# Attention branches D, B and C: where a modulation sum, A's turned outputs and the next branch's operands stand in a step

## Chip, cores and metric

The kernel runs on one core of a Trainium2 chip. The metric is the device time of one execution in microseconds (us), as a median over runs. Engines are named as in the profile: PE is TensorE, DVE is VectorE, ACT is ScalarE, POOL is GpSimd and SP is the queue that starts the weight transfers.

## What is computed

Two layers of a hybrid backbone over 256 latent and 256 context tokens, all in float32. Of a layer this matters here:

```python
out_a = mlstm_output(h_lat, mo, m_norm_g)          # branch A: normalised, gated
out_b = global_attention(...)                      # B: RMS-normed, rotated q and k
out_c = window_attention(..., sink)                # C: rotated q and k, sink logits
out_d = neighbourhood_attention(..., rel_bias)     # D: bias by relative position
# merge_branches:
g = jax.nn.sigmoid(gate_raw.reshape(B, T, N_BRANCH, D_MODEL))
y = g[:, :, 0] * (branches[0] @ w_branch[0])
for i in range(1, N_BRANCH):
    y = y + g[:, :, i] * (branches[i] @ w_branch[i])
return y @ w_out
```

After it comes a mixture of 32 experts with a modulation of its own. The modulation row is `silu(c) @ w_mod + b_mod`, one row per layer, of which the blocks n = 4 to 11 (512 columns each) are worked out beside the attention branches.

## The kernel before

The branches of a layer run in the order A, D, B, C. A stage is a list of items: in D, B and C an item is a pair of heads by 128 queries, 16 items in layer 0 and 8 in layer 1 (which needs the 256 latent tokens alone). A stage has one step more than items. In step i the engines do the following, each in its own program order, tied by semaphores:

- PE: `turn(i-1)` transposes the probabilities of item i-1 (L1373), `scores(i)` (L1363) multiplies queries and keys of the next, then come "dense groups" that belong to no item, with `values(i-1)` (L1387) between their two halves.
- DVE: `peaks(i)` adds the bias (L2075; at some items of D after four operations at L2067) and takes the maxima (L2078, L2084), `normalise(i)` scales the exponentials (L2096, L2098), `outputs(i-1)` copies the item's result (L2106).
- ACT: `turned_copy(i-1)` (L1085), `exponentials(i)` (L1096), then `fill`, which evacuates the dense groups that are ACT's (L953).

The dense groups are spread over the steps by `due`: projections for the next branch (`gq`, `gkv` in D, `wq`, `wkv` in B; L1213), products of the previous branch's outputs with `w_branch` (`val`, L1327; evacuated by DVE at L1915 and L1917, or L1919 and L1921) and gates (`gate`, L1314; evacuated by ACT). They take turns in two PSUM banks: group g writes bank g modulo 2 and waits until group g-2 has been evacuated (`dense_free`). Every engine knows a group's number from `plan_dense`, which lists the groups in order. A step has one or two groups in layer 0 and two or three in layer 1.

Three pieces of work beside the items are what the change touches.

- **Modulation sums.** In B and C, DVE adds up `csil * w_mod` row by row at the end of each step (`accumulate`, L1941 and L1943, four operations a step). When a block is complete, `modulation_sum` lets PE add over the partitions (L1231), a dense group too, and `sum_rows` lets DVE add the bias row (L1959). In layer 0 they stand in steps 4, 8, 12 and 16 of B and of C, in layer 1 in steps 2, 4, 6 and 8.
- **A's outputs.** DVE ends A with a norm over its outputs (L1881 to L1895) and raises `o_ready`. PE's `out_transposed("A")` waits for it and transposes them (L1249, four groups in layer 0, two in layer 1), and ACT evacuates them to where D's `val` groups read them.
- **The next branch.** `prepare_normed(i)` in D and `prepare_plain(i)` in B let DVE square, norm and rotate the operands of B and of C (L2013, L2014, L2019 to L2030, L1976 to L1981) once they have been evacuated. From step 8 of D in layer 0, and from step 5 in layer 1, a step norms and rotates one operand part or two.

Of the kernel before, what the change touches and what calls it, by code (L numbers as in the profile page):

```python
# [31 lines left out]
D = 1024  # L32
# [93 lines left out]
HOLD = {"A": 2}  # L126
PAIRS = 4
# [54 lines left out]
def sums_at(l, b, i):  # L182

    return [j for j in range(len(sum_blocks(l, b))) if sum_span(l, b, j)[1] == i]
# [46 lines left out]
def plan_dense():  # L231

    order = []
    for l in range(L):
        qt = q_tiles(l)
# [3 lines left out]
        for b in STAGES:  # L239
            n = n_items(l, b)  # L240
            after = {"D": "B", "B": "C"}.get(b)
            for i in range(stage_steps(l, b)):
                if b == "A" and i < n and spread_head(l, i) is not None:
                    order += [(l, "cb", 2 * spread_head(l, i) + d) for d in range(2)]
                if after and i == n:
                    order += [(l, "qt" + after, t) for t in range(qt)] + [(l, "kt" + after, 0)]
                order += [(l, "sum" + b, j) for j in sums_at(l, b, i)]
                order += [(l,) + fill_groups(l, b)[k] for k in due(l, b, i)]
            if b == "A":
                order += [(l, "otA", t) for t in range(qt)]  # L250
# [22 lines left out]
def hybrid_moe_kernel(nc, ins, out):  # L273
# [3 lines left out]
    with ctx:  # L277
# [667 lines left out]
        def _(act):  # L945
# [12 lines left out]
            for l in range(L):  # L958
# [113 lines left out]
                out_transposed("A")  # L1072

                def attention(b, sqrt_at=None):
# [25 lines left out]
                    for i in range(n + 1):  # L1100
# [7 lines left out]
                        if i == n and b in "DB":  # L1108
                            operands_transposed("B" if b == "D" else "C")
                        fill(b, i)  # L1110
# [74 lines left out]
        def _(pe):  # L1185
# [34 lines left out]
            for l in range(L):  # L1220
# [128 lines left out]
                def pairs(b):  # L1349
# [41 lines left out]
                    for i in range(n + 1):  # L1391
# [6 lines left out]
                        for j in sums_at(l, b, i):  # L1398
                            modulation_sum(b, j)
                        groups = due(l, b, i)  # L1400
                        half = (len(groups) + 1) // 2
                        fill(b, groups[:half])
                        if i:
                            values(i - 1)
# [60 lines left out]
                out_transposed("A")  # L1465
# [231 lines left out]
        def _(dve):  # L1697
# [34 lines left out]
            for l in range(L):  # L1732
# [314 lines left out]
                def attention(b):  # L2047
# [60 lines left out]
                    for i in range(n + 1):  # L2108
                        if i < n:
                            peaks(i)  # L2110
                        if b == "D":
                            prepare_normed(i)
                        if b == "B":
                            prepare_plain(i)
                        if i < n:
                            normalise(i)
                        sum_rows(b, i)
                        groups = due(l, b, i)
                        half = (len(groups) + 1) // 2
                        fill(b, groups[:half])  # L2120
                        if i:
                            outputs(i - 1)
# [289 lines left out]
```

How the kernel before makes its waits and increments, by code:

```python
        def weights(eng, key):  # L630
            slot, count, width = BLOCK[key]
            eng.wait_ge(w_full[slot], count)
            return slot_view(slot, width)
# [1 line left out]
        def expert_weights(eng, l, slot, i, width):  # L636
            eng.wait_ge(w_full[slot], 16 * first_use[l, slot] + 16 * i)
            return slot_view(slot, width)
# [9 lines left out]
        def wait_alone(eng, *waits):  # L649
            for s, v in waits:
                eng.wait_ge(s, v)
            eng.sem_inc(passed, 1)
# [7 lines left out]
            def __call__(self, ins_):  # L661
                ins_.then_inc(self.s, 1)
                self.n += 1
                self.eng.wait_ge(self.s, self.n)
# [1 line left out]
        def dense_wait(eng, g):  # L666
            eng.wait_ge(dense_full, g + 1)
            return ps[g % N_DENSE]
# [4 lines left out]
        @block.sync  # L674
        def _(sp):
            sp.dma_start(craw[:, 0, :], ins["c"]).then_inc(c_loaded, 16)
            sp.dma_start(craw[:, 1, :], ins["c_ctx"]).then_inc(c_loaded, 16)
            sp.dma_start(X[0:HALF, :, :], ins["x"][0].rearrange("(t p) d -> p t d", p=HALF)).then_inc(x_loaded, 16)
            sp.dma_start(X[HALF:P, :, :], ins["ctx"][0].rearrange("(t p) d -> p t d", p=HALF)).then_inc(x_loaded, 16)
            for l in range(L):
                for dst, src, wait, arrived in blocks[l]:
                    if wait:
                        sp.wait_ge(*wait)
                    sp.dma_start(dst, src).then_inc(arrived, 16)
                def load_expert(c, e, par):
```

## Time and profile before

| | |
|---|---|
| median of 3 runs | 2915.06 us (2908.91 to 2915.38) |
| the profiled execution | 2908.26 us, span 2906.8 us |
| PE busy | 2524.3 us, 87% of the span |
| chain that ended last, by engine | PE 67%, DMA 16%, DVE 9% |
| DVE, ACT busy | 1059.6 and 487.1 us |
| granted TensorE clock, mean | 0.939 |

In the profiled execution the stages D, B and C of layer 0 lie between 400 and 952 us, those of layer 1 between 1925 and 2254 us. A row of the time line has start, length, engine, line and operation, and in brackets how long its engine sat idle before it and what released it. A matmul in float32 shows as two records, so eight products are `x16`.

### The profile page before, as it was taken

What the parts mean: (1) busy time and instruction counts of PE and PEld (TensorE: products, weight loads), DVE (VectorE), ACT (ScalarE), POOL (GpSimd) and SP (SyncE); (2) the same over time, 40 slices, a digit from 0 to 9 for tenths busy, and PEclk for the clock granted to TensorE, in tenths of its full rate; (3) what the DMA queues carried; (4) which work ended last, traced back from release to release, by engine and by line L of the source; (5) the groups of instructions that cost most, each with busy time, mean ns of one, the idle gap of its engine ahead of it and who ended that gap; (6) DMA issues with size and microseconds to landing.
All of it is one profiled execution on the core that took longest, in us unless ns stands there. A gap on an engine that the chain in (4) does not pass through costs nothing.

```text
span 2906.8 us, 45309 instructions
## 1 busy us (share of the span) xinstructions
PE 2524.3 (87%) x18912; PEld 1544.5 (53%) x18913; DVE 1059.6 (36%) x2421; ACT 487.1 (17%) x965; POOL 251.5 (9%) x426
## 2 busy tenths in 40 slices
PE   5999989998889859999999789998989758888871
PEld 2455545454444457777777456566666434444440
DVE  1206536256474322222222332435446422111115
ACT  1113222222221100101001112222222101101010
POOL 3000000000000011111111200000001021111111
PEclk9989999999999959999999998999999879999996
DMA  9181202132325439999999721122455659999992
GB/s 291 58 328 49 68 34 69 48 134 84 102 95 141 162 114 367 372 372 385 382 378 386 258 92 58 58 102 84 156 167 147 253 197 408 412 417 411 411 378 81
DMA packets 153888, 618.46 MB, mean 213 GB/s; under 512 B 17680, under 2 KB 22080, under 8 KB 136960
## 3 DMA queue, kind: packets, MB, share of 16 engines
q1 hardware_dynamic: 126944, 558.92, 51.2%
q0 software_dynamic: 21696, 37.26, 4.8%
q10 hardware_dynamic: 5152, 20.97, 1.8%
q8 instruction: 64, 1.05, 0.1%
q14 instruction: 32, 0.26, 0.0%
HBM read 600.12 MB, written 46.32 MB: 222 GB/s over the span
## 4 chain that ended last, share of the span: by engine, by line
PE 67%; DMA 16%; DVE 9%; issue 4%; ACT 2%; ACTq 1%; POOL 1%; SPq 0%; DVEq 0%; POOLq 0%
DMA ring<-in_e_down_dram 13%; PE bank L1565 12%; PE bank L1314 12%; PE bank L1213 10%; PE bank L1203 6%; PE score_banks L1582 4%; PE bank L1327 3%; PE score_banks L1602 3%; PE score_banks L1587 2%; PE bank L1484 2%; PE score_banks L1363 2%; PE turned_banks L1373 2%; PE bank L1387 2%; PE bank L1242 1%; PE bank L1548 1%
## 5 line engine op out<-in xcount | busy, mean ns | idle before, releaser
L1565 PEld LDWEIGHTS bank<-scr,ring 128*64 128x64 f32 x8192 | 341.2, 138 | 14.7 <-issue 14.7
L1565 PE MATMUL bank<-scr,ring 128*64 128x96 f32 x8192 | 347.4, 247 | 1.4 <-DVE scr L2258 1.2
L1314 PE MATMUL bank<-HT,ring 128*128 128x512 f32 (+1 forms) x1024 | 343.9, 491 | 0.0
L1213 PE MATMUL bank<-ring,HT 128*128 128x512 f32 (+1 forms) x800 | 303.7, 536 | 5.9 <-ACT ring L953 5.9
L1558 PE MATMUL bank<-ring,scr 128*64 128x256 f32 x2048 | 238.4, 386 | 43.2 <-DMA ring<-in_e_gate_dram 21.6
L1314 PEld LDWEIGHTS bank<-HT,ring 128*128 128x128 f32 x1024 | 190.7, 190 | 141.8 <-issue 129.4
L1213 PEld LDWEIGHTS bank<-ring,HT 128*128 128x128 f32 x800 | 151.8, 193 | 150.9 <-issue 138.2
L1558 PEld LDWEIGHTS bank<-ring,scr 128*64 128x64 f32 x2048 | 146.5, 139 | 138.1 <-DMA ring<-in_e_gate_dram 38.2
L1203 PE MATMUL bank<-HT,ring 128*128 128x512 f32 (+1 forms) x512 | 197.6, 545 | 5.1 <-ACT scr L953 3.6
L1602 PE MATMUL score_banks<-ring,scr 128*64 128x512 f32 x512 | 135.2, 676 | 37.8 <-DMA ring<-in_e_down_dram 36.2
L1203 PEld LDWEIGHTS bank<-HT,ring 128*128 128x128 f32 x512 | 97.7, 193 | 96.7 <-issue 90.6
L953 ACT ACTIVATE ring<-bank 128x512 f32<-128x512 f32 (+1 forms) x122 | 63.1, 521 | 501.1 <-PE bank L1314 274.8
L1166 ACT ACT_TABLE_LOAD x64 | 82.1, 1283 | 348.9 <-DVE scr L2276 170.7
L1166 ACT ACTIVATE scr<-bank 128x384 f32<-128x384 f32 (+1 forms) x64 | 28.0, 438 | 634.2 <-PE bank L1565 336.1
L1582 PE MATMUL score_banks<-ring,scr 128*64 128x512 f32 x512 | 116.9, 598 | 0.8 <-issue 0.8
L1943 DVE SCALAR_TENSOR_TENSOR scr<-ring,csil,scr 128x512 f32<-128x512 f32 x160 | 109.9, 744 | 0.2
L2276 DVE TENSOR_TENSOR scr<-scr,bank 128x384 f32<-128x384 f32 x32 | 17.7, 554 | 248.9 <-PE bank L1565 248.9
L1096 ACT ACTIVATE scr<-score_banks,nms 128x512 f32<-128x512 f32 (+1 forms) x144 | 87.0, 609 | 113.1 <-DVE nms L2084 113.1
L1548 PE MATMUL bank<-consts,scr 96*128 96x96 f32 (+1 forms) x512 | 71.5, 282 | 39.2 <-DMA scr<-h,idx 19.6
L1242 PE MATMUL bank<-ring,scr 128*128 128x512 f32 x128 | 64.0, 662 | 47.5 <-DMA ring<-in_w_mod_dram 27.2
L1373 PE MATMUL turned_banks<-consts,scr 128*128 128x128 f32 x480 | 71.0, 290 | 37.3 <-DVE scr L2098 37.2
L2078 DVE TENSOR_REDUCE nm<-score_banks 128x2 f32<-128x1024 f32 (+1 forms) x72 | 75.2, 1044 | 72.4 <-PE score_banks L1363 70.3
(243 smaller groups left out, 2727.0 us busy)
## 6 DMA issues: line engine op xcount, KB each, us to landing
ring<-in_e_up_dram SPq DMA_DIRECT2D x64, 2048.0 KB, 21.1
ring<-in_e_down_dram SPq DMA_DIRECT2D x64, 2048.0 KB, 19.8
ring<-in_e_gate_dram SPq DMA_DIRECT2D x64, 2048.0 KB, 19.9
ring<-in_w_in_dram SPq DMA_DIRECT2D x34, 2048.0 KB, 7.8
ring<-in_w_mod_dram SPq DMA_DIRECT2D x32, 1024.0 KB, 5.2
ring<-in_w_mod_dram SPq DMA_DIRECT2D x8, 2048.0 KB, 20.2
ys<-consts ACTq DMA_DIRECT2D x1, 12288.0 KB, 39.7
ys<-consts ACTq DMA_DIRECT2D x1, 8192.0 KB, 62.5
```

Of the source, the lines that this page charges most:

```text
L1166: act.activation(SE[:, 0:hw], ps[2][:, 0:hw], ACT.Silu).then_inc(sg_ready, 1)
L1203: m = pe.matmul(bank[:, 0:cols], w[:, k, j * P:j * P + P], HT[:, k, 0:cols], start=k == 0, stop=k == KT_D - 1)
L1213: m = pe.matmul(bank[:, 0:width], HT[:, k, t * P:t * P + P], w[:, k, 0:width], start=k == 0, stop=k == KT_D - 1)
L1242: m = pe.matmul(bank[:, :], cs[:, k, :], w[:, k, :], start=k == 0, stop=k == KT_D - 1)
L1314: m = pe.matmul(bank[:, 0:NQ], w[:, k, (ft % 4) * P:(ft % 4) * P + P], HT[:, k, 0:NQ], start=k == 0, stop=k == KT_D - 1)
L1373: m = pe.transpose(PT_[:, hf, k * P:k * P + P], PB[:, hf, k * P:k * P + P], ident)
L1548: m = pe.transpose(ps[k // 4][:, (k % 4) * cap:(k % 4) * cap + cap], xe[:, k, :], ident[0:cap, 0:cap])
L1558: m = pe.matmul(ps[bank][hf * HALF:hf * HALF + cap, 0:256], XTv[:, k, :], w[:, k, hf * 256:hf * 256 + 256], start=k == 0, stop=k == KT_D - 1)
L1565: m = pe.matmul(ps[bank][rows_, f * cap:f * cap + cap], w[:, k, f * P + hf * HALF:f * P + hf * HALF + HALF], XTv[:, k, :], start=k == 0, s ...
L1582: m = pe.matmul(ps[4][hf * HALF:hf * HALF + HALF, :], hv[:, f, 0:HALF], w[:, f, hf * 512:hf * 512 + 512], start=f == 0, stop=f == 3)
L1602: m = pe.matmul(ps[4][hf * HALF:hf * HALF + HALF, :], lhs, w[:, f, hf * 512:hf * 512 + 512], start=f == 0, stop=f == 3)
L1943: m = dve.scalar_tensor_tensor(out=acc, in0=x, scalar=c, in1=acc, op0=ALU.mult, op1=ALU.add)
```

## The change

In the program order of the three engines:

1. `modulation_sum` on PE stands behind the first half of a step's dense groups, where it stood ahead of all of them. On DVE `sum_rows` stands behind the first half of the evacuations as well.
2. `out_transposed("A")` leaves the end of A. On PE and ACT it stands in step 1 of D (`TURN_A = 1`), on PE behind `scores(1)` and on ACT behind `exponentials(1)`.
3. `prepare_normed` and `prepare_plain` stand behind `outputs(i-1)` on DVE, where they stood between `peaks(i)` and `normalise(i)`.

Nothing is added or removed; the queues of SP and POOL keep their order.

```diff
@@ plan_dense @@
+                if b == "D" and i == TURN_A:
+                    order += [(l, "otA", t) for t in range(qt)]
+                groups = [(l,) + fill_groups(l, b)[k] for k in due(l, b, i)]
+                half = (len(groups) + 1) // 2
+                order += groups[:half] + [(l, "sum" + b, j) for j in sums_at(l, b, i)] + groups[half:]
-                order += [(l, "sum" + b, j) for j in sums_at(l, b, i)]
-                order += [(l,) + fill_groups(l, b)[k] for k in due(l, b, i)]
-            if b == "A":
-                order += [(l, "otA", t) for t in range(qt)]
@@ ACT: out_transposed("A") ahead of attention("D") is gone; in attention(b), step i @@
                         if i == n and b in "DB":
                             operands_transposed("B" if b == "D" else "C")
+                        if b == "D" and i == TURN_A:
+                            out_transposed("A")
                         fill(b, i)
@@ PE: out_transposed("A") ahead of pairs("D") is gone; in pairs(b), step i @@
-                        for j in sums_at(l, b, i):
-                            modulation_sum(b, j)
+                        if b == "D" and i == TURN_A:
+                            out_transposed("A")
                         groups = due(l, b, i)
                         half = (len(groups) + 1) // 2
                         fill(b, groups[:half])
+                        for j in sums_at(l, b, i):
+                            modulation_sum(b, j)
                         if i:
                             values(i - 1)
                         fill(b, groups[half:])
@@ DVE: attention(b), step i @@
                         if i < n:
                             peaks(i)
+                            normalise(i)
+                        groups = due(l, b, i)
+                        half = (len(groups) + 1) // 2
+                        fill(b, groups[:half])
+                        sum_rows(b, i)
+                        if i:
+                            outputs(i - 1)
                         if b == "D":
                             prepare_normed(i)
                         if b == "B":
                             prepare_plain(i)
-                        if i < n:
-                            normalise(i)
-                        sum_rows(b, i)
-                        groups = due(l, b, i)
-                        half = (len(groups) + 1) // 2
-                        fill(b, groups[:half])
-                        if i:
-                            outputs(i - 1)
```

Where A ends and D begins in layer 0, PE has these rows before (the 24 products are A's last gates, L1213 is the group `gq` 0, then `gq` 1):

```order
L1314 MATMUL bank<-HT,ring 128x512 x24
L1249 MATMUL bank<-consts,scr 128x128 x16
L1363 MATMUL score_banks<-ring 128x512 x2
L1213 MATMUL bank<-ring,HT 128x512 x8
L1373 MATMUL turned_banks<-consts,scr 128x128 x8
L1363 MATMUL score_banks<-ring 128x512 x2
L1213 MATMUL bank<-ring,HT 128x512 x8
L1387 MATMUL bank<-scr,ring 64x128 x8
```

and these now:

```order
L1317 MATMUL bank<-HT,ring 128x512 x24
L1366 MATMUL score_banks<-ring 128x512 x2
L1216 MATMUL bank<-ring,HT 128x512 x8
L1376 MATMUL turned_banks<-consts,scr 128x128 x8
L1366 MATMUL score_banks<-ring 128x512 x2
L1252 MATMUL bank<-consts,scr 128x128 x16
L1216 MATMUL bank<-ring,HT 128x512 x8
L1390 MATMUL bank<-scr,ring 64x128 x8
```

The sixteen transposes of A's outputs have moved behind the scores of item 1, and stay ahead of `gq` 1 and of the values of item 0.

On ACT the same place reads, before:

```order
L1071 ACTIVATE small<-small 128x16
L953 ACTIVATE ring<-bank 128x4x128 x4
L1096 ACT_TABLE_LOAD
L1096 ACTIVATE scr,rsum<-score_banks,nms 128x512 x2
L953 ACTIVATE scr<-bank 128x512
L1085 ACTIVATE scr<-turned_banks 128x1024
L1096 ACTIVATE scr,rsum<-score_banks,nms 128x512 x2
L953 ACTIVATE scr<-bank 128x512
```

and now:

```order
L1073 ACTIVATE small<-small 128x16
L1097 ACT_TABLE_LOAD
L1097 ACTIVATE scr,rsum<-score_banks,nms 128x512 x2
L955 ACTIVATE scr<-bank 128x512
L1086 ACTIVATE scr<-turned_banks 128x1024
L1097 ACTIVATE scr,rsum<-score_banks,nms 128x512 x2
L955 ACTIVATE ring<-bank 128x4x128 x4
L955 ACTIVATE scr<-bank 128x512
```

The four evacuations of A's transposes now stand behind the second pair of exponentials, those of item 1.

In step 5 of D in layer 1, DVE has these rows now, from the maxima of item 5 on (before, the two rows of `normalise`, here L2100 and L2102, stood behind both rotated parts):

```order
L2088 TENSOR_SCALAR nms<-nm 128x2
L2100 RECIPROCAL rden<-rsum 128x2
L2102 TENSOR_SCALAR scr<-scr,rden 128x512 x2
L1919 SCALAR_TENSOR_TENSOR ring<-ring,bank 128x256
L1921 COPY scr<-ring 128x256
L2110 COPY scr<-bank 128x128
L2026 RECIPROCAL small<-small 128x40
L2033 TENSOR_TENSOR scr<-scr,small 128x512
L2034 TENSOR_TENSOR scr<-scr,qk_g 128x512
L1980 TENSOR_TENSOR scr<-scr,consts 128x256
```

The second `val` group of the step is evacuated behind all sixteen operations of the two parts, as before; the first one and `outputs` now come ahead of them.

## Rows read from the trace of the kernel before

**Rows 1.** What PE waited for, whole span: total us, times, longest.
```profile
PE turned_banks L1373 <- DVE scr L2098: 37.2, 18, 6.2
...
PE bank L1231 <- DVEq L1948: 26.3, 11, 2.8
```

**Rows 2.** Time line, layer 0, from A's last product to the values of item 0.
```profile
400.04 3.77 PE L1249 MATMUL bank<-consts,scr 128*128 128x128 f32 x16 [11.66 <-DVEq L1897]
401.19 0.60 ACT L953 ACTIVATE ring<-bank 128x512 f32<-128x512 f32 x1 [10.65 <-PE bank L1249]
...
404.92 7.13 PE L1213 MATMUL bank<-ring,HT 128*128 128x512 f32 x16
405.04 2.33 DVE L2067 SCALAR_TENSOR_TENSOR scr<-scr,consts 128x384 f32<-128x384 f32 x4 [5.11 <-PE score_banks L1363]
...
409.40 0.17 DVE L2084 TENSOR_SCALAR nms<-nm 128x2 f32<-128x2 f32 x1
...
412.22 1.10 PE L1373 MATMUL turned_banks<-consts,scr 128*128 128x128 f32 x8 [0.17 <-DVE scr L2098]
...
421.38 1.09 PE L1387 MATMUL bank<-scr,ring 128*64 128x128 f32 x16
```

**Rows 3.** The same stretch in layer 1.
```profile
1925.48 1.97 PE L1249 MATMUL bank<-consts,scr 128*128 128x128 f32 x8 [6.84 <-DVEq L1897]
...
1929.39 14.18 PE L1213 MATMUL bank<-ring,HT 128*128 128x512 f32 x32
...
1944.37 1.13 PE L1363 MATMUL score_banks<-ring 64*128 64x512 f32 x4
1945.43 3.72 PE L1213 MATMUL bank<-ring,HT 128*128 128x256 f32 x16
1949.08 1.09 PE L1387 MATMUL bank<-scr,ring 128*64 128x128 f32 x16
1949.18 0.39 ACT L953 ACTIVATE scr<-bank 128x256 f32<-128x256 f32 x1
```

**Rows 4.** Time line, layer 0, D's step 8.
```profile
483.13 0.17 DVE L2084 TENSOR_SCALAR nms<-nm 128x2 f32<-128x2 f32 x1
...
487.55 0.88 DVE L2098 TENSOR_SCALAR scr<-scr,rden 128x512 f32<-128x512 f32 x2
...
488.49 1.97 PE L1373 MATMUL turned_banks<-consts,scr 128*128 128x128 f32 x8 [5.54 <-DVE scr L2098]
```

**Rows 5.** Time line, layer 1, D's step 5 and the first products of step 6.
```profile
1994.20 0.17 DVE L2084 TENSOR_SCALAR nms<-nm 128x2 f32<-128x2 f32 x1
...
2003.28 1.97 PE L1373 MATMUL turned_banks<-consts,scr 128*128 128x128 f32 x8 [6.24 <-DVE scr L2098]
2005.17 2.08 PE L1363 MATMUL score_banks<-ring 64*128 64x512 f32 x4
```

**Rows 6.** Time line, PE: sums in steps with projections or gates.
```profile
626.23 1.08 PE L1231 MATMUL bank<-scr,consts 128*64 128x512 f32 x4 [1.45 <-DVEq L1948]
...
695.53 1.08 PE L1231 MATMUL bank<-scr,consts 128*64 128x512 f32 x4 [2.63 <-DVEq L1948]
...
2117.79 3.47 PE L1231 MATMUL bank<-scr,consts 128*64 128x512 f32 x4 [2.58 <-DVEq L1948]
...
2222.18 1.93 PE L1231 MATMUL bank<-scr,consts 128*64 128x512 f32 x4
```

**Rows 7.** Time line, layer 0: step 8 of B, then step 4 of C.
```profile
661.52 1.08 PE L1231 MATMUL bank<-scr,consts 128*64 128x512 f32 x4 [2.84 <-DVEq L1948]
662.53 3.70 PE L1327 MATMUL bank<-scr,ring 128*128 128x512 f32 x8
664.70 0.88 DVE L2098 TENSOR_SCALAR scr<-scr,rden 128x512 f32<-128x512 f32 x2
...
805.51 0.88 DVE L2098 TENSOR_SCALAR scr<-scr,rden 128x512 f32<-128x512 f32 x2
...
806.45 1.09 PE L1373 MATMUL turned_banks<-consts,scr 128*128 128x128 f32 x8
```

More of the change, by code:

```diff
@@ L126 @@
 HOLD = {"A": 2}
+TURN_A = 1
 PAIRS = 4
@@ L1071, in _ @@
                 act.activation(hss[:, 0:4 * qt], hss[:, 0:4 * qt], ACT.Sqrt).then_inc(hstd_ready, 1)
-                out_transposed("A")
                 def attention(b, sqrt_at=None):
@@ L1464, in _ @@
                 attention()
-                out_transposed("A")
                 evacuated(G[l, "nv", 3])
```

## Prediction

> **What bounds the kernel now.** The page's busy table puts PE at 87% of the span, and its chain that ended last is PE's for 67%; so I read in the attention stages what ends PE's waits. The list of waits has two large entries there: the turn of the probabilities waits for `normalise` 18 times, 37.2 us in all, and the modulation sum waits 11 times, 26.3 us, for DVE to finish `accumulate` [rows 1]. The time line adds the two waits for A's norm, 11.66 us in layer 0 and 6.84 us in layer 1 [rows 2, 3]. The reader is to see in it, step by step, which of two loops is longer. One is PE's own work. The other runs through DVE: `accumulate`, `peaks`, then ACT's exponentials, `normalise`, the `val` evacuations, and `accumulate` again. Only where PE's own work is the longer loop is a wait ahead of the sum worth its length.
>
> **A's outputs, layer 0.** PE is done with A at 400.04 - 11.66 = 388.4. Now it goes on with scores(0) (1.1) and `gq` 0 (7.13) [rows 2] and is free at 396.6. DVE ends the norm at 400.0 as before and can start item 0's `peaks` at once; from their first operation to the turn it takes 412.22 - 405.04 = 7.2 us [rows 2], so turn(0) comes at 407.2 and PE has idled 10.6 us, little less than before. After a wait of 5.54 us the turn took 1.97 us [rows 4], and the scores behind a like one 2.08 [rows 5], near twice their length at full clock (1.10 [rows 2], 1.13 [rows 3]); with both, scores(1) end at 411.2. Then come the transposes, and here something is late that was not: their evacuations stand behind `exponentials(1)` on ACT. In layer 1 ACT was free for the next evacuation 1949.18 - 1944.37 = 4.8 us after scores(1) began [rows 3], 3.7 us after they ended. Two groups of transposes find free banks, the third and fourth wait for an evacuation of 0.60 us [rows 2] each, and `gq` 1 for a third. So `gq` 1 starts some 5.7 us behind the scores, at 416.9, and the values of item 0 start at 424.0 where they started at 421.38 [rows 2]. That is 2.6 us lost; I add 0.6 for half clock after the new wait: **+3.2** (bounds: 0, if the evacuations slip in earlier, to +4.5, if `gq` 1 runs slow).
>
> **A's outputs, layer 1.** PE is free at 1918.6 and has both `gq` groups, 14.18 us [rows 3], to do: until 1933.7. DVE is through at 1925.4 and item 0 is normalised at 1932.6, so that the wait of 6.84 us goes altogether. Turn and scores put the start of scores(1) at 1934.7; `gkv` 0 needs the bank of the first transposes, evacuated 4.8 + 0.6 us later, so it starts at 1940.2, and the values 1949.08 - 1945.43 = 3.65 us after that, at 1943.9 against 1949.08 [rows 3]: 5.2 us won. With 0.6 for the clock after this new wait of 3.4 us: **-4.6** (-6.8 to -3).
>
> **The prepared operands.** From the negated maxima (L2084) to the turn, item 0 took 412.22 - 409.40 = 2.8 us [rows 2]. In D's step 8 of layer 0 it took 5.4, since 4.1 us of norm and rotation lay between [rows 4]; now the turn comes 2.5 us earlier. But the same 4.1 us then stand ahead of the next `peaks`, and ahead of the second `val` evacuation, and steps 9 to 11 bring such parts again: I keep 1.0 of the 2.5, and 0.4 from a short wait of the same kind in step 3: **-1.4** (-3 to +1). In layer 1, step 5 holds two parts, and the turn comes at 1994.20 + 2.8 = 1997.0 instead of 2003.28 [rows 5]. That is 6.3 us, and 2.0 of half clock on turn and scores go too. Late next is the step's second `val` group: it is evacuated behind both parts (16 operations and a reciprocal, 7.8 us in the time line), at about 2006.2, and the second gate of step 6 needs its bank, where PE arrives at 2002.8. That gives back 3.4 us of wait, 0.2 for ACT behind the exponentials and 0.5 for the clock: **-4.2** (-8.3 to -1). The parts moved in B delay the `peaks` behind them by up to 0.3 us in layer 0 and 0.7 in layer 1: **+1.0** (0 to +4).
>
> **The sums.** Where the step has projections or gates, PE's loop is the longer one, as 7.13 us a group in layer 0 [rows 2] covers DVE's accumulation; the wait goes at full length. There are four of these in layer 0, two of 1.45 us, one of 2.63 and one of 2.5, and one in layer 1, 2.58 us, with a sum that ran at half clock behind it, 3.47 against 1.93 [rows 6]; I take 3.8 for that, 11.8 in all. In step 8 of B in layer 0 the sum waited 2.84 us, and the turn then stood at 666.8; but `normalise` ended at 664.70 + 0.88 = 665.6 [rows 7], so no more than about 1.0 is to be had. Together **-12.8** (-14 to -8). In C, steps 4 and 8 of layer 0, `normalise` ends at 805.51 + 0.88 = 806.39 and the turn starts at 806.45 with no wait of PE's own between [rows 7]. DVE's loop was as long as PE's with its wait; the wait only moves from ahead of the sum to ahead of the turn. The three such steps of layer 1 are alike, with 0.3 us each for a shorter queue: **-1.0** (-6 to +2).
>
> SP's and POOL's queues keep their order. The weights that they bring are released by PE's groups and come earlier with them; the sums that come last are followed by all of C's last value products, which cover the loading of the finished row.
>
> The sum is 3.2 - 4.6 - 1.4 - 4.2 + 1.0 - 12.8 - 1.0 = -19.8 us, on 2908.3 of the profiled execution: 2888.5. The runs of before lie at 2909 once and at 2915 twice, the profile beside the lower one; so the median may come out up to 7 us above this sum. I predict **2891 us**.
>
> **A rule weighed against rows.** Waits of 5.54 and 6.24 us were followed by half clock (1.2 GHz) for about two rows of PE, costing 2 us [rows 4, 5]. For shorter ones the rows disagree: behind 2.63 and 2.84 us in layer 0 the sum ran at full length, 1.08 us [rows 6, 7], behind 2.58 us in layer 1 at near half, 3.47 for 1.93 [rows 6]. So I charge the new waits a third of that price. The Trainium skill, "TensorE: Matmul & The Clock Gate", section "HAM oscillation — how this bites in real kernels", speaks against the change here: waits that recur between bursts send PE back to the low clock each time. By that rule each of the moved waits would cost the whole 2 us, and the sum would come near -8.
>
> **Rivals.**
>
> 1. Forecast, as summed, -12 to -28 us: 2880 to 2896, and up to 7 more for the level of the runs. Chance 0.62.
> 2. *The waits go at full length.* DVE's loop gets slack too, since it no longer stands between `peaks` and `normalise`. All 26.3 us of sum waits and 1.5 us of clock for each of three in layer 1 go, the two in D (5.5 and 6.2, with 2 each of clock), and layer 1's A; layer 0's A costs 3.2: 26.3 + 4.5 + 15.7 + 4.6 - 3.2 = 48 us, 2860; anything past 28 us counts here. For it: the waits ahead of the sums are the second entry of the list. Against it: 806.39 and 806.45. Chance 0.13.
> 3. *The clock takes it back.* Some eight waits of 2.4 to 3.5 us stand in new places (one in each layer's step 1, one in D's step 6, five ahead of a turn or a bank in value steps), each followed by 2 us: the 16 less what is in the sum leave -8, 2900. Chance 0.09.
> 4. *The waits reappear ahead of the turn everywhere*, in gate steps too, so that the change does not do what it says for the sums. Only D's -7.0 and B's +1.0 are left: -6, 2902. Against it: 7.13 us a gate group is longer than the 4 us from the maxima to the turn's release. Chance 0.11.
> 5. *Slower: C's value steps of layer 0 fall to half clock altogether.* Place: its eight steps with one `val` group, where PE now does all of a step's work in one run and then idles. That work is 1.1 + 1.1 + 3.70 + 1.1 = 7 us at full clock and 14 at half, against a loop of about 9 us: some 5 us a step. It decides from six of the eight steps on (over 8.7 + 19.8 us); all eight give +20, 2928. For it: layer 1's 3.47. Against it: layer 0's sums at full clock behind the same waits. Chance 0.05.
>
> **The numbers.** A change of 0.3%, 8.7 us, is about what a measurement of this kernel can tell from none. Faster by more: rivals 1 and 2 and some of 3 and 4, **0.80**. Within: most of 3 and 4, **0.15**. Slower: **0.05**. The range of 2870 to 2905 us holds the forecast with its bounds, the nearer half of rival 2 and rivals 3 and 4, and leaves out the rest of 2, and 5. The forecast's own range is 2880 to 2903.
>
> **What would show it.** In the profile after: layer 0's wait ahead of item 0's turn near 10.6 us, a wait of 3 to 4 us for ACT inside A's transposes, and the same in layer 1 ahead of `gkv` 0, with none ahead of turn(0). No wait ahead of turn(5) of D in layer 1, but one of 3 us and more ahead of the second gate behind it, released by DVE. No wait for `accumulate` ahead of sums in gate steps; in C's value steps a wait of about 2.5 us ahead of the turn where none was. I am wrong if the value steps get shorter, if ACT evacuates A's transposes ahead of the exponentials, or if PE's rows in C take twice their length.

## The result, and the profile of the changed kernel

The changed kernel took 2895.6 us, the median of 12 runs (2891.2 to 2906.2), beside 2911.6 us for the kernel before (12 runs, 2907.0 to 2918.6). The ratio is 0.9947, with a 95% interval of 0.9934 to 0.9960: 15.4 us less (12 to 19), or 0.5%, by the ratio. A second set of runs (the last experiment below) gave 0.9940 (0.9922 to 0.9958). The forecast was 2891 us in a range of 2870 to 2905.

The profiled execution has a span of 2890.0 us against 2906.8. Of these 16.8 us, 4.7 are there before the first changed instruction: TensorE is done with A at 383.7 where it was at 388.4. What is left to explain in this pair of traces is 12.1 us.

What PE waited for over the whole span (line numbers are 2 to 4 higher than before; total us, times, longest), to be held against [rows 1]:

```profile
PE turned_banks L1376 <- DVE scr L2102: 45.4, 23, 10.8
...
PE bank L1495 <- DMA ring<-in_w_out_dram: 7.1, 1, 7.1
PE bank L1330 <- DVE ring L1923: 5.9, 2, 2.9
...
PE bank L1234 <- DVE ring L1923: 3.5, 1, 3.5
PE bank L1317 <- DVE ring L1919: 3.3, 1, 3.3
...
PE bank L1234 <- DVEq L1952: 1.3, 2, 0.7
```

The sum's wait for `accumulate` has gone from 26.3 us to 1.3. But the turn's has grown from 37.2 us to 45.4, and three entries are new, waits for a bank that DVE evacuates (L1923 and L1919 are the two forms of a value group's evacuation). The total of the named waits hides where they lie, so the time line comes next.

Time line of PE, layer 0, from A's end to the values of item 0 ([rows 2] before):

```profile
383.67 1.13 PE L1366 MATMUL score_banks<-ring 64*128 64x512 f32 x4
384.73 7.13 PE L1216 MATMUL bank<-ring,HT 128*128 128x512 f32 x16
402.69 1.97 PE L1376 MATMUL turned_banks<-consts,scr 128*128 128x128 f32 x8 [10.83 <-DVE scr L2102]
404.59 2.08 PE L1366 MATMUL score_banks<-ring 64*128 64x512 f32 x4
406.60 1.34 PE L1252 MATMUL bank<-consts,scr 128*128 128x128 f32 x8
410.91 1.97 PE L1252 MATMUL bank<-consts,scr 128*128 128x128 f32 x8 [2.97 <-ACT ring L955]
412.80 7.68 PE L1216 MATMUL bank<-ring,HT 128*128 128x512 f32 x16
420.41 1.09 PE L1390 MATMUL bank<-scr,ring 128*64 128x128 f32 x16
```

The wait for A's norm is gone, and one of 10.83 us stands ahead of the first turn. From A's end to the values it is 420.41 - 383.67 = 36.7 us, where [rows 2] give 33.0: 3.7 us lost. The same stretch in layer 1 ([rows 3] before):

```profile
1908.18 1.13 PE L1366 MATMUL score_banks<-ring 64*128 64x512 f32 x4
1909.24 14.00 PE L1216 MATMUL bank<-ring,HT 128*128 128x512 f32 x32
1923.08 1.04 PE L1376 MATMUL turned_banks<-consts,scr 128*128 128x128 f32 x8
1924.04 1.13 PE L1366 MATMUL score_banks<-ring 64*128 64x512 f32 x4
1925.10 1.09 PE L1252 MATMUL bank<-consts,scr 128*128 128x128 f32 x8
1929.49 5.37 PE L1216 MATMUL bank<-ring,HT 128*128 128x256 f32 x16 [3.30 <-ACT ring L955]
1934.80 1.09 PE L1390 MATMUL bank<-scr,ring 128*64 128x128 f32 x16
```

Here nothing is waited for ahead of the turn, since two `gq` groups cover DVE. The stretch takes 26.6 us instead of 30.4: 3.8 us won. Behind the 3.30 us wait a group of 3.72 us takes 5.37.

Layer 1, D's steps 5 and 6 ([rows 5] before):

```profile
1982.99 1.09 PE L1376 MATMUL turned_banks<-consts,scr 128*128 128x128 f32 x8
1984.01 1.13 PE L1366 MATMUL score_banks<-ring 64*128 64x512 f32 x4
1985.07 3.72 PE L1317 MATMUL bank<-HT,ring 128*128 128x256 f32 x16
1992.13 6.47 PE L1317 MATMUL bank<-HT,ring 128*128 128x256 f32 x16 [3.34 <-DVE ring L1919]
```

The 6.24 us ahead of turn(5) are gone. The second gate behind it waits 3.34 us for a value group's bank and then takes 6.47 us for 3.72, most of it at half clock.

Layer 1, B's step 4 and C's step 2, each with its sum (L1234) between value groups (L1330). The sum shows as x3, since its fourth record lies behind two of the values' records:

```profile
2084.20 2.79 PE L1234 MATMUL bank<-scr,consts 128*64 128x512 f32 x3 [3.49 <-DVE ring L1923]
...
2161.65 1.50 PE L1234 MATMUL bank<-scr,consts 128*64 128x512 f32 x3 [0.66 <-DVEq L1952]
...
2167.41 2.77 PE L1330 MATMUL bank<-ring 128*128 128x256 f32 x8 [2.95 <-DVE ring L1923]
```

And the end of layer 1's attention, which no row ahead of the prediction shows. First the kernel before: SP's issue of `w_out`, PE's first products with it, and the first of POOL's last three reads, two of the modulation and one of a norm's weights:

```profile
2253.79 1.00 SPq L686 DMA_DIRECT2D ring<-in_w_out_dram  x2
2271.14 22.48 PE L1491 MATMUL bank<-ring,scr 128*64 128x512 f32 x96 [3.56 <-DMA ring<-in_w_out_dram]
...
2250.24 0.53 POOL L827 DMA_DIRECT2D scr<-mod  x1 [1.35 <-DMA mod<-scr]
```

Then the changed kernel:

```profile
2235.83 1.00 SPq L688 DMA_DIRECT2D ring<-in_w_out_dram  x2
2256.74 22.71 PE L1495 MATMUL bank<-ring,scr 128*64 128x512 f32 x96 [7.13 <-DMA ring<-in_w_out_dram]
...
2236.08 0.53 POOL L829 DMA_DIRECT2D scr<-mod  x1 [1.35 <-DMA mod<-scr]
```

The view of DMA issues gives KB each and the us from the issue to the landing, before:

```profile
ring<-in_w_out_dram SPq DMA_DIRECT2D x2, 2048.0 KB, 13.9
...
scr<-mod POOLq DMA_DIRECT2D x1, 768.0 KB, 6.0
```

and in the changed kernel:

```profile
ring<-in_w_out_dram SPq DMA_DIRECT2D x2, 2048.0 KB, 17.7
...
scr<-mod POOLq DMA_DIRECT2D x1, 768.0 KB, 10.5
```

POOL's three reads (1.5 MB) were issued 3.5 us ahead of `w_out` and are now issued 0.3 us behind it. The last row of the modulation is finished 3.8 us later against the gates' end, since its sum stands behind the first of them. `w_out` (2 x 2 MB) is used 20.9 us after its issue and not 17.4, and PE waits 3.6 us more.

Step by step (from the start of one item's scores to the next) the two traces differ as follows. Steps not named agree within 0.1 us, or differ by clock alone. The 1.9 us of B's step 4 are shared out by experiment 3, where 0.7 of them came with the sums alone.

| where | what | measured, us | forecast, us |
|---|---|---|---|
| layer 0, A's end to D's values | A's outputs | +3.7 | +3.2 |
| layer 1, the same | A's outputs | -3.8 | -4.6 |
| layer 0, D's values to B's scores | prepared operands | -2.1 | -1.4 |
| layer 1, the same | prepared operands | -2.0 | -4.2 |
| B, both layers | prepared operands (0.6 + 0.4 + 1.1) | +2.1 | +1.0 |
| gate and projection steps, B's step 8 | sums: 1.7, 1.7, 2.9, 2.5, 1.1; 4.3 in layer 1; five small ones, 1.0 | -15.2 | -12.8 |
| value steps | sums: C of layer 0 +0.2, C of layer 1 +1.3, B's step 4 +0.7 | +2.2 | -1.0 |
| ahead of `w_out` | sums | +3.6 | 0 |
| sum | | -11.5 | -19.8 |

The two long stretches outside this table hold no changed instruction, and in this pair they differ by +1.9 us (from the first product with `w_out` in layer 0 to A's end in layer 1) and -2.4 us (from the first product with `w_out` in layer 1 to the end). The 12 traces spread wider than that there: 965.5 to 970.8 us and 633.3 to 639.3 us.

### The profile page after: what moved, and what is told of

Its sections match the earlier page's. It is cut to its first block, busy times and chain, and to the rows that moved or that the text cites. A ratio compares the mean times of both kernels' runs of the same rounds, so it can differ in the third digit from the quotient of the medians.

```text
span 2890.0 us, 45296 instructions
## 1 busy us (share of the span) xinstructions
PE 2521.1 (87%) x18912; PEld 1545.1 (53%) x18913; DVE 1060.8 (37%) x2421; ACT 486.0 (17%) x965; POOL 251.9 (9%) x426
## 4 chain that ended last, share of the span: by engine, by line
PE 66%; DMA 16%; DVE 10%; issue 4%; ACT 2%; ACTq 1%; POOL 1%; SPq 0%; DVEq 0%; POOLq 0%
DMA ring<-in_e_down_dram 13%; PE bank L1569 12%; PE bank L1317 12%; PE bank L1216 10%; PE bank L1206 7%; PE score_banks L1586 4%; PE score_banks L1606 3%; PE bank L1330 2%; PE score_banks L1591 2%; PE bank L1488 2%; PE score_banks L1366 2%; PE turned_banks L1376 2%; PE bank L1390 1%; PE bank L1245 1%; PE bank L1552 1%
## 5 line engine op out<-in xcount | busy, mean ns | idle before, releaser
L1216 PE MATMUL bank<-ring,HT 128*128 128x512 f32 (+1 forms) x800 | 306.2, 540 | 10.8 <-ACT ring L955 10.8
L1606 PE MATMUL score_banks<-ring,scr 128*64 128x512 f32 x512 | 138.3, 689 | 38.4 <-DMA ring<-in_e_down_dram 36.7
L1376 PE MATMUL turned_banks<-consts,scr 128*128 128x128 f32 x480 | 70.9, 290 | 45.4 <-DVE scr L2102 45.4
L1330 PE MATMUL bank<-ring 128*128 128x512 f32 (+1 forms) x256 | 97.3, 527 | 11.5 <-DVE ring L1923 5.9
L1245 PE MATMUL bank<-ring,scr 128*128 128x512 f32 x128 | 62.7, 651 | 44.8 <-DMA ring<-in_w_mod_dram 26.3
## 6 DMA issues: line engine op xcount, KB each, us to landing
ring<-in_w_mod_dram SPq DMA_DIRECT2D x8, 2048.0 KB, 20.9
```

The costliest lines, as they stand in the source:

```text
L1216: m = pe.matmul(bank[:, 0:width], HT[:, k, t * P:t * P + P], w[:, k, 0:width], start=k == 0, stop=k == KT_D - 1)
L1330: m = pe.matmul(bank[:, 0:NQ], wb[:, k, ft * P:ft * P + P], OT[b][:, k, 0:NQ], start=k == 0, stop=k == 3)
L1376: m = pe.transpose(PT_[:, hf, k * P:k * P + P], PB[:, hf, k * P:k * P + P], ident)
L1606: m = pe.matmul(ps[4][hf * HALF:hf * HALF + HALF, :], lhs, w[:, f, hf * 512:hf * 512 + 512], start=f == 0, stop=f == 3)
```

## Experiments

All times are ratios to the kernel before on the same chip, with a 95% interval. The first three each make one part of the change alone.

**1. A's outputs alone.** The edit, on the kernel before (TensorE's side; ACT and the order of banks follow):

```diff
                 attention()
-                out_transposed("A")
...
+                        if b == "D" and i == 1:
+                            out_transposed("A")
                         for j in sums_at(l, b, i):
                             modulation_sum(b, j)
```

> The kernel before with one part of the change: A's outputs are turned in D's second step. By the terms on record this part is worth +3.2 us in layer 0 and -4.6 us in layer 1, so -1.4 us against before; by the two traces at hand (A's last scores to the first values of D: 33.0 us before and 36.7 after in layer 0, 30.4 and 26.6 in layer 1) it is +3.7 and -3.8, so 0 us. Both say a ratio of 0.9995 to 1.000. A rival: the layer-1 saving depends on the clock being high there, and without the other parts it is not kept; then the ratio is 1.001 to 1.0015. In the profile: a wait of about 3 us for ACT inside A's transposes in both layers, and about 10.8 us ahead of the first turn of D in layer 0.

Measured: 1.0004 (0.9995 to 1.0013). The waits are as expected: 10.83 us ahead of the first turn, 3.21 and 3.30 us for ACT inside the transposes, 3.7 us for `w_out`. From A's end to the scores of D's item 2 it took 39.9 us in layer 0 and 32.2 in layer 1, where the kernel before took 35.0 and 36.0: +4.8 (1.1 of it in rows that ran slower than in the changed kernel's trace) and -3.8. But for those rows this part gives in layer 1 what it costs in layer 0, as the terms from the traces say; the forecast's -1.4 (0.9995) is at the interval's edge.

**2. The prepared operands alone.**

```diff
                         if i < n:
                             peaks(i)
-                        if b == "D":
-                            prepare_normed(i)
...
                             outputs(i - 1)
+                        if b == "D":
+                            prepare_normed(i)
+                        if b == "B":
+                            prepare_plain(i)
```

> The kernel before with one part of the change: DVE prepares the next branch's operands behind the step's outputs. Terms on record: -1.4 us in layer 0's D, -4.2 us in layer 1's D, +1.0 us in B, so -4.6 us (ratio 0.9984). By the traces at hand D's stretches from values(0) to B's first scores became 2.1 and 2.0 us shorter, so about -4 us with little in B. Rival: in layer 1 the wait that goes from the turn of step 5 comes back whole ahead of the second gate behind it (3.3 us and a step at half clock), and the part is worth under 1.5 us (ratio 0.9995 or more).

Measured: 0.9997 (0.9988 to 1.0005), so no gain, as the rival has it, but not by its mechanism: D became 4.4 us shorter (2.1 and 2.3) as the first theory says, and B became 4.6 us longer. In layer 1's B a wait came up that neither trace had shown. The rows are from this experiment's time line:

```profile
2066.90 0.17 DVE L2098 RECIPROCAL rden<-rsum 128x2 f32<-128x2 f32 x1 [1.51 <-ACT scr L1098]
...
2073.35 2.74 DVE L1945 SCALAR_TENSOR_TENSOR scr<-ring,csil,scr 128x512 f32<-128x512 f32 x4
...
2076.20 1.93 PE L1233 MATMUL bank<-scr,consts 128*64 128x512 f32 x4 [2.03 <-DVEq L1950]
```

Between `peaks` and `normalise` DVE waits for ACT's exponentials. Before, the preparation stood in that time. Now DVE idles there, 1.51 us in step 1, and does the preparation later. From `peaks` to the accumulation of the row, at the end of step 1, it is 9.4 us where it was 7.1, and the sum at the head of step 2 waits for that. In the changed kernel the sum stands behind two groups of 3.6 us and that wait does not exist. The parts are therefore not additive: moving the sums spares 2 us of what moving the preparation costs. The rest of B's loss is 1.0 us of the waits that the changed kernel has as well, and 1.7 us in layer 0's step 8 at half clock, which is chance (last section).

**3. The sums alone.**

```diff
-                        for j in sums_at(l, b, i):
-                            modulation_sum(b, j)
                         groups = due(l, b, i)
                         half = (len(groups) + 1) // 2
                         fill(b, groups[:half])
+                        for j in sums_at(l, b, i):
+                            modulation_sum(b, j)
```

> The kernel before with one part of the change: the modulation row's sums behind the first dense groups of their step. Terms on record: -12.8 us in the steps of gates and projections, -1.0 us in the steps of values, so -13.8 us (ratio 0.9953). By the traces at hand B and C became 5.3, 4.0 and 2.5 us shorter and C of layer 1 0.8 us longer, so -11.0 us (0.9962). If the three parts add up, the ratios of the three single runs multiply to about 0.9947. Rival: the parts need one another (a wait that one takes away comes back at the next), and the three together give less than 0.9947 alone, that is their product is 0.996 or more. A second rival: w_out arrives later because the gates of C end sooner, as in the changed kernel (7.1 us of waiting against 3.6), and takes 3.5 us of it back; then its wait is near 7 us here too, and near 3.6 us in the other two runs.

Measured: 0.9956 (0.9944 to 0.9968), 12.8 us. The three ratios multiply to 0.9957, against 0.9947 and 0.9940 for all parts together; the intervals do not tell these apart, but the difference has the sign of the 2 us above. The wait for `w_out` is 7.8 us here, and 3.7 and 3.5 in the two runs without moved sums, as the second rival said: it belongs to the sums. Whether by its mechanism, experiment 4 tells. So nearly all of the change's gain is this part.

**4. The last sum of layer 1 ahead of its gates again.** This and the four that follow start from the changed kernel. A function says how many of a step's groups stand ahead of its sum, for PE, for DVE and for the order of banks:

```diff
+def cut(l, b, i):
+    groups = due(l, b, i)
...
+    return 0 if l == L - 1 and b == "C" and i == n_items(l, b) else (len(groups) + 1) // 2
```

> The changed kernel with the last sum of layer 1 (C, step 8) ahead of its gates again, as before. Theory: with the sum behind the first gate the last row of the modulation is written about 3.7 us later against the gates' end, so GpSimd's three reads of the modulation (1.5 MB) are issued 0.3 us behind w_out's load instead of 3.5 us ahead of it, and share the DMA engines with it: w_out lands 17.7 us after its issue where it took 13.9. Put back, TensorE's wait for w_out falls from 7.1-7.8 us to about 3.6 us, and the step itself costs nothing (the sum waited 0 us in the kernel before): -3.5 us against the changed kernel. Rival: w_out comes later because the gates end sooner, whatever GpSimd does; then the wait stays over 7 us.

Measured: 0.9932 (0.9909 to 0.9954), against 0.9947; an interval of this width cannot show 3.5 us, but the rows do:

```profile
2233.98 0.53 POOL L836 DMA_DIRECT2D scr<-mod  x1 [1.36 <-DMA mod<-scr]
...
2237.53 1.00 SPq L695 DMA_DIRECT2D ring<-in_w_out_dram  x2
...
2254.98 22.52 PE L1504 MATMUL bank<-ring,scr 128*64 128x512 f32 x96 [3.67 <-DMA ring<-in_w_out_dram]
```

The reads are 3.55 us ahead again and the wait is 3.67. Counted from the scores of item 7 the gates end within 0.4 us of where they end in the changed kernel, so the rival falls. PE comes to `w_out` 3.1 us sooner, 38.0 us behind those scores instead of 41.1: the 3.5 us, less 0.3 that the sum costs ahead of the gates. The cause is that the reads and `w_out` share the DMA engines. From 4 us behind `w_out`'s issue to its use these are busy without a gap, with a share of 0.99 to 1.06 in the three traces, so no transfer fits in free of charge. The view of DMA issues says the same from the other side: POOL's read of 768 KB takes 6.2 us here, near the 6.0 of the kernel before and not the 10.5 of the changed one. The Trainium skill, "DMA: Bandwidth & Descriptors", section "Queues, rings and completion order", has each DMA engine take turns between the queues that have work for it, packet by packet. The traces agree as far as they go: with both in flight neither waits for the other's end, and both become slower. The turns by packet themselves are not shown.

**5. The sums of layer 1's steps with values alone ahead again.**

```diff
+    vals = all(fill_groups(l, b)[k][0][:3] == "val" for k in groups)
+    return 0 if l == L - 1 and vals else (len(groups) + 1) // 2
```

> The changed kernel with the sums of layer 1 that fall into steps with values alone (B step 4, C steps 2 and 4) ahead of them again. Theory: DVE frees a value group's bank only behind the normalisation, so TensorE can run two dense groups behind the scores and the third waits for DVE; the sum behind the first groups is one more of them (3.5 us in B step 4, 2.95 us in C steps 2 and 4, and rows at half clock). Ahead of them the sum falls back to its wait for the accumulation (2.6 us): the three steps go from 16.6, 13.9 and 13.9 us to 14.7, 12.3 and 13.0 us, C step 3 gives back 0.9: -3.4 us against the changed kernel. Rival: with the prepared operands behind (they end later now) the accumulation is later too, and B step 4 stays at 16 us or more: -1.6 us or less.

Measured: 0.9947 (0.9931 to 0.9964), not told from the changed kernel; 3 us are 0.1%, less than this interval can show. In the trace B's step 4 went from 16.55 to 14.77 us and C's steps 1 to 4 from 43.8 to 42.5: -3.1 us, where -3.4 was expected. The profiled execution does not show it in its span, since other stretches with the same instructions came out longer (3.1 us until A's end, 5 us behind the start of C's item 7, and between these 5.6 us in layer 0 and its experts). The mechanism holds: behind the scores two dense groups find free banks, since DVE evacuates value groups only after `normalise`; a sum between them is the third.

**6. DVE's preparation last of all.**

```diff
                         fill(b, groups[half:])
+                        if b == "D":
+                            prepare_normed(i)
+                        if b == "B":
+                            prepare_plain(i)
```

> The changed kernel with DVE's preparation of the next branch behind the second half of its value groups too, that is last of all in a step but the row's accumulation. Theory: in layer 1's D the second gate of step 6 waits 3.3 us because its bank is freed by a value group that DVE takes only behind the preparation, and the step then runs at half clock (20.07 us against 15.19 in the kernel before). With the preparation behind it the wait goes and the step takes 15 to 16.5 us: -3.5 to -5 us against the changed kernel, nothing elsewhere. Rival: the clock, not the bank, is what is slow there (it fell behind step 4's wait for the bias); then the wait goes and under 2 us of the step's length with it. Second rival: DVE has no room in the step at all, and the wait reappears ahead of the turn of step 6 at full length: 0.

Measured: 0.9962 (0.9950 to 0.9974); no gain, if anything a loss. Expected -3.5 to -5 us; step 6 of D in layer 1 became 3.3 us shorter, B's step 3 1.7 us longer and its step 4 0.9 shorter, D's step 10 in layer 0 0.9 longer. And the wait in step 6 did not go. It moved one group on, to another releaser:

```profile
1995.41 7.17 PE L1317 MATMUL bank<-HT,ring 128*128 128x256 f32 x32
2002.52 1.09 PE L1390 MATMUL bank<-scr,ring 128*64 128x128 f32 x16
2006.62 3.69 PE L1317 MATMUL bank<-HT,ring 128*128 128x256 f32 x16 [3.01 <-ACT ring L955]
```

Both gates now find their banks, and the third waits for ACT, which evacuates gates behind its exponentials. Of the 3.3 us that were won, the wait gives 0.3 and nearly all the rest is half clock (the second gate took 6.47 us before). None of the three theories has this as the next wait.

**7. Short accumulations in C.** All operations of `accumulate` in C but the first of each sum work on 64 of 512 columns; the other columns are left out of the modulation's sum.

```diff
+                        if b == "C" and k:
+                            acc, x = acc[:, 0:64], x[:, 0:64]
```

> The changed kernel with the accumulation of the modulation row in stage C on 64 of its 512 columns (all but the first operation of each sum), so that DVE's loop is about 2 us shorter per step with the same waits and transfers; the rows' other columns are left out of the sum. Theory: the waits ahead of the turn in the steps with values of C (11 to 12 us in layer 0, 2 us in layer 1) stand there because DVE's loop of a step (peaks, normalisation, value group, outputs, accumulation) is longer than TensorE's; with thin rows they vanish and C's first nine steps in layer 0 become 9 to 12 us shorter. Rival: what is waited for is the chain from scores over ACT to the normalised block (5.34 us in step 0, where nothing is accumulated), and the waits stay above half of their length; then under 5 us.

Measured: 0.9886 (0.9866 to 0.9906). The steps 1 to 8 of C in layer 0 took 55.7 us instead of 67.4 (-11.7), steps 1 to 4 in layer 1 36.7 instead of 43.8 (-7.1). In layer 0 the turns of items 2, 3 and 4 had waits of 1.10, 1.97 and 1.24 us in the changed kernel's time line:

```profile
781.25 0.66 PE L1376 MATMUL turned_banks<-consts,scr 128*128 128x128 f32 x4 [1.10 <-DVE scr L2102]
...
788.72 0.66 PE L1376 MATMUL turned_banks<-consts,scr 128*128 128x128 f32 x4 [1.97 <-DVE scr L2102]
789.31 1.99 PE L1366 MATMUL score_banks<-ring 64*128 64x512 f32 x4
...
798.40 1.09 PE L1376 MATMUL turned_banks<-consts,scr 128*128 128x128 f32 x8 [1.24 <-DVE scr L2102]
```

and the first two have none in this one's, the third 0.68 us:

```profile
783.87 0.66 PE L1376 MATMUL turned_banks<-consts,scr 128*128 128x128 f32 x4
...
789.30 0.66 PE L1376 MATMUL turned_banks<-consts,scr 128*128 128x128 f32 x4
```

The first two waits stood there in the kernel before as well (1.10 and 1.97 us); the third, in the step of the sum, is the one that the change put in the place of the sum's 2.63. So C's value steps are bound by DVE's loop, accumulation included, and moving the wait for the sum in them can win nothing: the prediction's reading of [rows 7].

**8. A's outputs turned in D's first step.** TensorE turns them behind the step's first dense group, and ACT evacuates that group and the turned outputs ahead of `exponentials(0)`:

```diff
-TURN_A = 1
+TURN_A = 0
...
+                        half = (len(due(l, b, i)) + 1) // 2
+                        early = b == "D" and i == TURN_A
+                        if early:
+                            fill(b, i, slice(0, half))
+                            out_transposed("A")
                         if i < n:
                             exponentials(i)
```

> The changed kernel with A's outputs turned in D's first step behind its first dense group, and ACT copying that group and the turned outputs ahead of the first exponentials. Theory: in layer 0 TensorE idles 10.8 us ahead of D's first turn, because DVE finishes A's outputs (at 395.3) and only then the peaks; the transposes (3.3 us) need nothing later than 395.3 and fit into that wait, and ACT is idle from 387 to 400. Then D's second step loses its transposes and the 3.0 us wait in them: -6.2 us in layer 0. In layer 1 the transposes (1.1 us) lie between the two groups of the first step, and the 3.3 us wait ahead of the next projection goes, with part of its half clock: -3 to -5 us. Sum -9 to -11 us against the changed kernel, near 2885 us at its level, a ratio of 0.991 to before. Rival: ACT reaches the exponentials later, turn(0) slips by the copies (2.5 us in layer 0), and the gain is 5 us or less. Second rival: TensorE's clock falls after the longer run of other waits, and nothing over 3 us is left.

Measured: 2885.6 us, 0.9913 (0.9899 to 0.9928), as expected. The time line of layer 0:

```profile
387.01 7.13 PE L1220 MATMUL bank<-ring,HT 128*128 128x512 f32 x16
397.68 1.09 PE L1256 MATMUL bank<-consts,scr 128*128 128x128 f32 x8 [3.54 <-DVEq L1905]
399.02 1.97 PE L1256 MATMUL bank<-consts,scr 128*128 128x128 f32 x8 [0.25 <-ACT ring L956]
405.56 1.97 PE L1380 MATMUL turned_banks<-consts,scr 128*128 128x128 f32 x8 [4.56 <-DVE scr L2106]
```

The transposes lie inside the former wait of 10.8 us. From D's first scores to those of its item 2 it is 32.5 us instead of 38.8 in layer 0 (-6.3) and 27.6 instead of 32.2 in layer 1 (-4.5). Turn(0) comes 0.6 us later, not the 2.5 of the rival. Steps 4 to 6 of layer 1's D came out 2.2 us shorter too, mostly by the clock: the gate behind the wait there, 3.33 us, took 5.38 us and not 6.47.

**9. Repairs 4, 5 and 8 together, and 6 in layer 1's D alone.**

> The changed kernel with four repairs together: A's outputs turned in D's first step (10.8 us by the trace of that run), the sums of layer 1's steps with values alone ahead again (3.1 us), the last sum ahead again (3.5 us), and DVE's preparation last of all in layer 1's D (3.3 us). If each trace's steps add up: -20.7 us against the changed kernel, near 2875 us, a ratio to before of 0.987 to 0.989. Rival: the repairs overlap, as the three parts of the change did in B of layer 1, or TensorE's clock takes part of it back, and it stays above 2881 us (0.9895 or more).

Measured: 2877.4 us, 0.9887 (0.9870 to 0.9905), within the ratio expected and 18 us less than the changed kernel. By steps it is 18.2 us: 9.5 (experiment 8 had 10.8; rows behind the first turn were slower here), 3.6 (5), 3.5 at `w_out` (4), and 1.6 from step 6 of D instead of 3.3, since the wait for ACT was followed by half clock here, with 5.38 us for the 3.69 above. Of these 1.6 us experiment 8 had 1.1 without this repair, so that it adds 0.5 here. The repairs add up but for that clock.

**10. The changed kernel again.**

> The changed kernel itself once more, so that what its profile shows ahead of the changed part can be told from the change: its first profile reached the end of A 4.7 us earlier than that of the kernel before, in the same instructions. If that is chance, this profile's end of A lies anywhere between 383 and 392 us (the runs so far had 384.7 to 389), and the ratio is again 0.9935 to 0.996. Rival: it belongs to the kernel; then the end of A comes at 383.5 to 384.5 again.

Measured: 0.9940 (0.9922 to 0.9958); A ended at 386.4 us and the span was 2901.1, 11.1 us more than in the first profile of the same program. The rival falls. Over all traces A's end lies between 383.7 and 388.4 us, and the pair that the result was read from holds both ends.

## Why the prediction held, and where it was off

The time came out 4.6 us above the forecast, inside its range and that of its first case (2880 to 2903). That it came so near is in part luck: the terms measured -11.5 us where the forecast had -19.8, and taken from the median before, 2911.6, they would have given 2900. Term by term:

- **A's outputs.** Both signs and sizes held: +3.7 for +3.2 and -3.8 for -4.6. The turn came after 10.8 us of idling (10.6 forecast), and the waits for ACT inside the transposes were 2.97 and 3.30 us (3 to 4). The clock behind the wait in layer 1 (the 3.30 us) was priced at 0.6 and cost 1.65 (5.37 for 3.72).
- **Prepared operands.** In layer 0 the wait of D's step 8 fell from 5.54 to 3.01 us, the 2.5 forecast, and the clock gave 0.9 more. Steps 9, 10 and the last two gave back 1.7 in all: -2.1 for -1.4. In layer 1 the order of events was right: no wait ahead of turn(5), one of 3.34 us ahead of the second gate, released by DVE (3.4 forecast). The clock behind it was mis-sized: 0.5 was charged, and the gate took 6.47 us for 3.72, 2.75 more. That is the gap from -4.2 to -2.0. In B the price was 2.1, not 1.0, inside its bound of 4. The prediction had priced it as a delay of `peaks` by up to 0.3 and 0.7 us, and left out that the preparation had stood in DVE's wait for ACT; where a step of B holds two parts, DVE's accumulation comes 2.3 us later (experiment 2). By itself this part was worth nothing (experiment 2); the sum of terms did not say that its price in B hangs on the sums being moved.
- **Sums in gate and projection steps.** "The wait goes at full length" held in each: -15.2 for -12.8. Three of the four steps of layer 0 gave the wait and 0.2 us more, the fourth the wait alone, layer 1's 4.3 for 3.8, B's step 8 1.1 for 1.0, and small steps without a wait another 1.0.
- **Sums in value steps.** "The wait only moves from ahead of the sum to ahead of the turn" held in layer 0 (+0.2 over C's steps 1 to 8), and experiment 7 shows why. The new waits ahead of the turn, in the two steps of a sum, are 1.24 and 1.29 us and not 2.5; half clock took the rest, with scores of 1.99 us for 1.13 and a value group of 4.49 for 3.70 in the first of them. "The three such steps of layer 1 are alike" failed. These steps have two and three value groups, and the sum takes the second bank from them; the price was +2.0 us there, and experiment 5 gives that and more back.
- **The queues.** "The sums that come last are followed by all of C's last value products, which cover the loading of the finished row" failed. The row was in time, as forecast. But its reads moved from ahead of `w_out`'s load to beside it, and that load is waited for: +3.6 us, shown by experiment 4.

Errors of -3.1 us in two terms and +11.4 in the others make -11.5 of the -19.8; the pair of profiles has -12.1 behind A's end. By the ratio the medians show -15.4 (-19 to -12). The 4 us between are not placed: profiles of one and the same program differ by more (experiment 10).

The rule of the Trainium skill on recurring waits ("TensorE: Matmul & The Clock Gate", section "HAM oscillation — how this bites in real kernels"), which the prediction weighed, held in part. In layer 1 the two new waits of 3.30 and 3.34 us were followed by rows at half clock. In C of layer 0 half clock followed the waits of 1.97 us (scores of 1.99 us for 1.13, in the rows of experiment 7), but not those of 1.10 and 2.93; in the kernel before the same scores took 1.13 us behind the same 1.97. No stage fell to half clock altogether, so the rival that ended slower did not come. The prediction's -8 us for this rule is not what its terms give: its sum of -19.8 names 1.7 us for the clock behind new waits, and 16 us in their place make -5.5.

## What to carry to other kernels

When a wait is moved behind other work, count the banks and not only the time: the moved product is one more group in flight, and what it takes a bank from may be evacuated by the very engine that is late. Look up what the moved step's result feeds, transfers included, and what is issued beside them: a row that comes in time can still put 1.5 MB beside a load on the critical path. A wait for an engine is also a place. In layer 0 the transposes of A's outputs, which need nothing that ends late in it, cost 0.6 us inside the 10.8 us wait and 6.9 us one step later, where the evacuating engine was busy. The same holds for work that already stands in such a wait: DVE's preparation did, and to take it out put DVE 2.3 us behind in one step.

## What the runs showed of the hardware

In the attention stages most steps repeat within 0.1 us from run to run, except where TensorE's granted clock changes between its two levels (1.2 and 2.4 GHz). Which rows run at the lower one behind a wait varies between executions. Experiment 1 left B as it was before, so its step 8 in layer 0 can be held against [rows 7]: after the same wait of 2.84 us the sum took 1.98 us instead of 1.08 and the value group 5.89 instead of 3.70.

```profile
665.92 1.98 PE L1234 MATMUL bank<-scr,consts 128*64 128x512 f32 x4 [2.84 <-DVEq L1952]
667.83 5.89 PE L1330 MATMUL bank<-scr,ring 128*128 128x512 f32 x8
```

The step lasted 13.3 us there, 11.9 in experiment 2 and 10.2 before, with the same instructions of PE in the same order. With a handful of such places a program's time moves by several us, so a single pair of profiles cannot be read closer than that in total, while a step at one clock can be read to 0.1 us.
